# Routing on the normalised rows ahead of gain and bias, and a head whose first two weight units run in pairs

## The reference, cut to what matters

```
x  = layer_norm(x, emb_ln_g, emb_ln_b)
m  = token_mixer(x)        # z = x @ w_in + b_in: attention, spatial gating, convolution; gates; w_o
x1 = layer_norm(ALPHA * x + m, ln1_g, ln1_b)
s  = sigmoid(x1 @ w_router)                    # 16 experts
sb = (s + b_router) in 4 groups of 4
group = argmax(sum of the best 2 of sb)        # one group per token
idx   = best 2 experts of that group
w     = s[idx] / sum(s[idx])
y  = sum over the 2 experts of w * ((silu(x1 @ w_e1) * (x1 @ w_e3)) @ w_e2)
out = layer_norm(ALPHA * x1 + y, ln2_g, ln2_b)
```

## Time and profile before

| | |
|---|---|
| median of 3 runs | 828.07 us (827.59 to 828.2) |
| the profiled execution | 827.32 us, span 825.5 us |
| TensorE matmul busy | 750.6 us, 91% of the span |
| VectorE, ScalarE, GpSimd busy | 628.9, 426.8, 94.6 us |
| mean granted TensorE clock | 0.959 of full |

### The profile page before, as it was taken

How to read it: one execution, slowest core, us unless ns; L and a number is a source line. 1 busy time by engine, 2 the same in 40 slices (tenths; PEclk the granted TensorE clock), 3 DMA queues, 4 the chain that set the end, 5 groups by cost and what they waited for, 6 DMA issues and landing times.

```text
span 825.5 us, 10954 instructions
## 1 busy us (share of the span) xinstructions
PE 750.6 (91%) x3544; PEld 617.0 (75%) x3544; DVE 628.9 (76%) x902; ACT 426.8 (52%) x569; POOL 94.6 (11%) x91
## 2 busy tenths in 40 slices
PE   3899999999999999999999649999999999999930
PEld 3688877888888888888888438888888888888720
DVE  4589986666588658434578658999999999999948
ACT  4622134547322246232321508888888888888711
POOL 3100000000000000000113310111111111112606
PEclk9899999999999999999999859999999999999965
DMA  8833657221323332333596627999999999996252
GB/s 256 241 93 93 193 146 197 70 60 53 95 83 102 102 98 81 104 96 97 191 371 234 250 97 244 362 349 367 368 379 365 388 376 372 370 370 230 82 202 104
DMA packets 129103, 171.95 MB, mean 208 GB/s; under 512 B 15338, under 2 KB 67270, under 8 KB 129046
## 3 DMA queue, kind: packets, MB, share of 16 engines
q1 hardware_dynamic: 121440, 154.95, 55.5%
q0 software_dynamic: 6688, 15.79, 5.5%
q10 hardware_dynamic: 934, 0.69, 0.3%
HBM read 164.05 MB, written 15.97 MB: 218 GB/s over the span
## 4 chain that ended last, share of the span: by engine, by line
PE 78%; DVE 11%; DMA 4%; ACT 3%; issue 2%; SPq 2%; ACTq 0%; POOL 0%; DVEq 0%; POOLq 0%
PE bank L1642 23%; PE bank L1643 23%; PE bank L1644 23%; PE bank L1855 2%; DMA raw<-in_w_in_dram 2%; DVE w_lo L940 2%; SPq L561 1%; DVE conv L1004 1%; PE bank L1818 1%; DVE conv_odd L1004 1%; PE bank L1680 1%; PE bank L1870 1%; DMA w_s_in<-in_w_s_dram 1%; PE bank L1690 1%; PE bank L1637 1%
## 5 line engine op out<-in xcount | busy, mean ns | idle before, releaser
L940 DVE TENSOR_TENSOR w_lo<-raw,w_hi 128x1024 fp32r<-128x1024 f32 x104 | 126.3, 1220 | 81.2 <-ACT w_hi L670 80.7
L670 ACT CAST w_hi<-raw 128x1024 fp32r<-128x1024 f32 x104 | 108.2, 1049 | 105.6 <-PE bank L1644 92.6
L1642 PE MATMUL bank<-xT_hi,w_hi 128*128 128x512 f32 x352 | 138.6, 394 | 1.1 <-DVE vs L1093 1.0
L1643 PE MATMUL bank<-xT_lo,w_hi 128*128 128x512 f32 x352 | 137.5, 391 | 0.0
L1644 PE MATMUL bank<-xT_hi,w_lo 128*128 128x512 f32 x352 | 137.3, 390 | 0.0
L1642 PE MATMUL bank<-w_hi,xgT_hi 128*128 128x512 f32 x192 | 79.1, 412 | 1.6 <-DVE xgT_lo L1392 1.6
L1642 PEld LDWEIGHTS bank<-xT_hi,w_hi 128*128 128x128 f32 x352 | 66.4, 189 | 15.7 <-issue 2.1
L1644 PEld LDWEIGHTS bank<-xT_hi,w_lo 128*128 128x128 f32 x352 | 66.4, 188 | 14.0
L1644 PE MATMUL bank<-w_hi,xgT_lo 128*128 128x512 f32 x192 | 76.7, 400 | 0.0
L1643 PE MATMUL bank<-w_lo,xgT_hi 128*128 128x512 f32 x192 | 76.4, 398 | 0.0
L1643 PEld LDWEIGHTS bank<-xT_lo,w_hi 128*128 128x128 f32 x352 | 66.4, 189 | 13.4
(11 more groups left out here) (251 smaller groups left out, 1582.5 us busy)
## 6 DMA issues: line engine op xcount, KB each, us to landing
raw_more<-in_w_e_dram SPq DMA_DIRECT2D x48, 512.0 KB, 6.7
raw<-in_w_e_dram SPq DMA_DIRECT2D x48, 512.0 KB, 7.0
raw_late<-in_w_e_dram SPq DMA_DIRECT2D x48, 512.0 KB, 6.4
raw_rows<-in_w_e_dram SPq DMA_DIRECT2D x48, 512.0 KB, 7.2
raw<-in_w_in_dram SPq DMA_DIRECT2D x28, 512.0 KB, 5.6
raw<-in_w_gate_dram SPq DMA_DIRECT2D x24, 512.0 KB, 3.7
raw<-in_w_o_dram SPq DMA_DIRECT2D x8, 512.0 KB, 3.8
x_scratch<-x_in SPq DMA_DIRECT2D x4, 512.0 KB, 6.7
```

The lines of the kernel that those rows point to most:

```text
L670: act.copy(hi_slot(j), raw_slot(j)).then_inc(hi_cast, 1)
L940: dve.tensor_tensor(lo_slot(j), raw_slot(j), hi_slot(j).bitcast(F32), ALU.subtract).then_inc(lo_cast, 1)
L1642: pe.matmul(out, hi_l, hi_r, start=start, stop=False)
L1643: pe.matmul(out, hi_l, lo_r, start=False, stop=False)
```

## The change

*Head.* The six weight units are issued without a wait for the rows. `ln1_g` and `ln1_b` are loaded as rows too, on GpSimd's queue, and `w_s` has a semaphore of its own. TensorE turns chunks 0 to 6 of the first two tiles before it waits for the rows. VectorE makes both parts of unit 0; the high parts of x's odd chunks are made by VectorE, those of even chunks by ScalarE. The first two outputs use banks 0 and 1, and their units are run chunk by chunk in turns; `w_s` is turned behind them. SyncE no longer waits for the stored x and `w_s` before the bias loads.

*Routing.* ScalarE writes the normalised rows to a new tile `x1n`; the transposes and the router read that, with `w_router` multiplied by `ln1_g` and a row `ln1_b @ w_router` added. The transposes of the first tiles stand between the `w_o` products of the later ones. The scores come out with tokens on partitions: the turned rows are the stationary operand, 16 columns move. All of `ln1_g` and `ln1_b` is applied by VectorE beside that. `router_bias` is eight matmuls of 16 columns, `route` one and eight. Ranks come from tables of pairwise comparisons that don't wait for each other, summed by one reduction. Between the two casts ahead of the routing stand six small VectorE operations (clearings, constants, `info[..., 0]`). The position counts are float32r. Two of the four expert casts are moved behind the routing. GpSimd's passes (`ln1_b`, ALPHA) are gone; ALPHA is taken in VectorE's first of the two last adds (L1482).

```
-        sp.wait_ge(rows_loaded, 16 * 9)
-                sp.wait_ge(x0_stored, 16 * TT)
-                sp.wait_ge(*drained("w_s"))
...
-        cast_hi(0)
         act.wait_ge(*drained("vectors"))
...
-            if c:
+            if c % 2:
                 act.wait_ge(x0T_full, c)
-                act.copy(xT_hi[:, c - 1, :], conv[:, (c - 1) % WC, :]).then_inc(x0T_hi_done, 1)
+                act.copy(xT_hi[:, c - 1, :], conv[:, (c - 1) % WC, :]).then_inc(x0T_hi_act, 1)
+            if c == 1:
+                cast_hi(1)
...
+        dve.tensor_copy(hi_slot(0), raw_slot(0)).then_inc(first_hi, 1)
+            if c % 2:
+                dve.wait_ge(x0T_full, c + 1)
+                dve.tensor_copy(xT_hi[:, c, :], conv[:, c % WC, :]).then_inc(x0T_hi_dve, 1)
...
+        first_units(0, (0, 1))
+        first_units(1, (0, 1))
+        for c in range(2, DC):
+            for u in range(2):
+                first_units(u, (c,))
+        pe.wait_ge(w_s_loaded, 16)
         turn("w_s", lambda k: w_s[:, k, :])
...
+        normalise(0)
+        normalise(1)
+        copy_x1T(0)
+        normalise(2)
+        copy_x1T(1)
+        normalise(3)
+        cast_hi(U_MOE)
+        copy_x1T(2)
+        cast_hi(U_MOE + 1)
+        copy_x1T(3)
         act.wait_ge(*filled("router"))
+        act.activation(r_s[:].rearrange("p t g e -> p (t g e)"), bank("router")[:, 0:TT * EXPERTS],
+                       ACT.Sigmoid).then_inc(frees("router"), 1)
+        cast_hi(U_MOE + 2)
+        cast_hi(U_MOE + 3)
...
         def scale_x1(t):
-            if t % 2:
+            dve.wait_ge(normalised, 2 * t + 2)
+            dve.tensor_tensor(x1[:, t, :], x1n[:, t % 2, :], ln1_g[:], ALU.mult).then_inc(scaled, 1)
+            dve.tensor_tensor(x1[:, t, :], x1[:, t, :], ln1_b[:], ALU.add).then_inc(x1_ready[t], 1)
...
         def ranks(rank, beats, value):
             for d in range(1, 4):
                 k = 4 - d
+                over = 5 * (k - 1) + 1
+                dve.tensor_tensor(beats[:, :, 4 * d:4 * d + over:5], value[:, :, 0:k], value[:, :, d:4], ALU.is_ge)
+                dve.tensor_tensor(beats[:, :, d:d + over:5], value[:, :, d:4], value[:, :, 0:k], ALU.is_gt)
+            dve.wait_ge(dve_step, step(6))
+            dve.tensor_reduce(rank, beats.rearrange("p m (i j) -> p m i j", j=4), AX.X, ALU.add)
...
+        cast_lo(U_MOE)
...
+        cast_lo(U_MOE + 1)
...
         make_onehot(0, 0)
         make_onehot(1, 1)
         slot_tokens(0, 0, None, keep=False)
         slot_tokens(1, 1, None, keep=False)
+        cast_lo(U_MOE + 2)
+        cast_lo(U_MOE + 3)
...
+        mix_out(0)
+        mix_out(1)
+        router_bias()
+        mix_out(2)
+        turn_x1(0)
+        mix_out(3)
+        turn_x1(1)
+        route(0)
+        turn_x1(2)
+        route(1)
+        turn_x1(3)
+        route(2)
+        route(3)
...
-        pe.matmul(bank("position")[:, 0:80], before, sel, start=True, stop=False)
+        pe.matmul(bank("position")[:, 0:80], before_r[:], sel, start=True, stop=False)
...
+        pool.wait_ge(x1_stored, 16 * TT)
         pool.memset(xg[:], 0.0).then_inc(pool_step, 1)
-        pool.wait_ge(x1_stored, 16 * TT)
...
-        for t in range(TT):
-            pool.tensor_scalar(x1[:, t, :], x1[:, t, :], ALPHA, None, ALU.mult).then_inc(x1_scaled, 1)
```

More of the change, by code:

```diff
@@ new lines, in _ @@
+        dve.tensor_scalar(token_one[:], token, 1.0, None, ALU.add).then_inc(dve_step, 1)
+        dve.tensor_copy(info[..., 0], tokens).then_inc(dve_step, 1)
+        cast_lo(U_MOE + 1)
+        dve.wait_ge(dve_step, step(6))
+        dve.wait_ge(*drained("router"))
+        dve.tensor_tensor(r_sb[:], r_s[:], per_tile(b_router[:]), ALU.add).then_inc(dve_step, 1)
+        dve.wait_ge(dve_step, step())
+        ranks(r_rank[:].rearrange("p t g e -> p (t g) e"), r_beats[:], r_sb[:].rearrange("p t g e -> p (t g) e"))
@@ L1328, in _ @@
[L1328 removed]
+        dve.tensor_tensor(r_kth[..., 3:4], r_kth[..., 2:3], sel[..., 2:3], ALU.add).then_inc(dve_step, 1)
+        dve.wait_ge(dve_step, step(2))
         dve.tensor_tensor(gates[:], r_tmp[:].rearrange("p t g e -> p t (g e)"),
                           w_inv[:].unsqueeze(2).to_broadcast([P] + by_expert), ALU.mult).then_inc(dve_step, 1)
[L1331 removed]
@@ L1332, in _ @@
-        dve.wait_ge(dve_step, step(3))
+        dve.scalar_tensor_tensor(out=info[..., 1], in0=r_kth[:].rearrange("p t g e -> p t (g e)"), scalar=float(T),
+                                 in1=token_one[:].unsqueeze(2).to_broadcast([P] + by_expert), op0=ALU.mult,
+                                 op1=ALU.add).then_inc(dve_step, 1)
+        dve.wait_ge(dve_step, step(2))
         dve.tensor_copy(info[..., 2], gates[:]).then_inc(dve_step, 1)
-        tt(info[..., 1], position[:], tokens, ALU.add)
+        dve.wait_ge(*filled("position"))
@@ L1346, in _ @@
-        dve.tensor_scalar(position[:], position[:], -1.0, None, ALU.add).then_inc(routed, 1)
+        dve.tensor_tensor(info[..., 3], gates[:], info[..., 2].bitcast(F32), ALU.subtract).then_inc(dve_step, 1)
         dve.wait_ge(routed, 1)
@@ new lines, in turn_x1, with route @@
+        def turn_x1(t):
+            for half in range(2):
+                pe.wait_ge(normalised, 2 * t + half + 1)
+                turn(("x1T", t, half), lambda k: x1n[:, t % 2, (4 * half + k) * P:(4 * half + k + 1) * P])
+        def route(t):
+            if t == 0:
+                open_bank("router")
+                pe.wait_ge(router_scaled, 4)
+                pe.wait_ge(*drained("router_bias"))
+            scores = bank("router")[:, t * EXPERTS:(t + 1) * EXPERTS]
+            pe.matmul(scores, ones[0:1, :], router_row[0:1, :], start=True, stop=False)
+            for half in range(2):
+                pe.wait_ge(*drained(("x1T", t, half)))
+                for c in range(4 * half, 4 * half + 4):
+                    o = pe.matmul(scores, x1T[:, c, tokens_of(t)], w_routed[:, c, :], start=False, stop=c == DC - 1)
+            if t == TT - 1:
+                o.then_inc(fills("router"), 1)
```

277 lines of the change are left out of this document (147 added, 130 removed).

## The result

The changed kernel takes 815.8 us (median of 4 runs, 814.27 to 817.13) against 827.83 beside it: a ratio of 0.9851, 95% interval 0.9838 to 0.9863. That is 12.0 us faster, inside the range of 807 to 817, 4.3 us above the forecast of 811.5, and outside the band of 808 to 814.5 that had the largest chance: it lies where the first rival had put it. The gain that the steps had summed to was 16.6. The profiled execution took 817.13 us, its span 815.3.

What follows compares the result with a forecast made beforehand. TensorE was taken as busy nearly throughout, leaving head, routing and end to give time: 827.3 - 6.0 (head) - 10.6 (routing) - 0 (end) = 810.7 us, as a median 811.5; 8-in-10 range 807 to 817.

Steps and rivals of the forecast that it cites:

- the first rival: Routing gives less: gather at loaded price (+3.4), comparisons 0.2 apart (+1.3) or router products at lower clock; 813 to 816, chance 0.13.
- Head: Ahead of unit 2: first matmul at 18.6 instead of 25.21 us, unit 2 at 31.2 instead of 37.5; -6.0 us.
- So the gain is carried along: Up to 437 us: TensorE had under 3 us of idle, so the head's 6.0 us would persist.
- The path to `r_sb`: Routing, last tile's variance to `r_sb`: ScalarE's casts and copies set the pace; start 466.1 instead of 473.34 us, -7.2.
- so I leave it at 0.23: Routing: each new router product takes 0.23 us, as the old ones did; 0.9 us for the last four.
- The root: Routing, after tile 3's variance: the root takes 1.0 us, from an undisturbed 0.55 rather than the 1.46 seen.
- Ranks and choice: Routing: `r_sb` to choice takes 3.0 us instead of 5.3 (-2.3); choice to one-hot 1.7 instead of 3.3 (-1.5).
- The gather: Routing, after one-hot: it took 3.4 us with quiet DMA and now meets the end of weight traffic; +0.4 us.
- (2): Head gives only 2 to 3 us: rows or x late behind weight units, or long low clock; 814.5 to 820, chance 0.12.
- (3): Head gives more: earlier bias loads remove part of 3 us idle, low clock costs nothing; 805 to 809, chance 0.10.
- (4): Experts are bound by DMA, not TensorE, so only the head's gain stays; 821, chance 0.04.
- (5): Slower: TensorE's clock stays low into the units, 0.2 us more per matmul; 831 if five units, chance 0.04.

Runs made afterwards that it cites:

- head only: Kernel before with only the change's edits ahead of unit 2, first layer norm and routing as before: 823.14 us, ratio 0.9943.
- copies first: Changed kernel with ScalarE copying tile 2's turned rows before normalising tile 3, and two expert casts moved later: 815.54 us, ratio 0.9850.
- fillers: Changed kernel with eight idle wide products added behind route(1), tile 3's turns and route(2): 817.49 us, ratio 0.9866.

## Why the forecast was right, and where it was off

Second profiles of both kernels, stage by stage, in us; the forecast's figures are those of its own steps:

| stage | forecast | measured |
|---|---|---|
| to unit 2 | -6.0 | -5.61 (36.91 to 31.30) |
| units 2 to 68 | 0 | +1.26 |
| unit 68 to tile 3's variance | +1.6 | +1.29 |
| variance to `r_sb` | -8.8 (16.95 to 8.1) | -2.88 (16.81 to 13.93) |
| `r_sb` to one-hot | -3.8 | -3.54 (8.61 to 5.07) |
| one-hot to first expert product | +0.4 | -0.16 |
| first 24 expert products | 0 | +0.84 |
| the other experts' products | 0 | -2.24 and -0.13 |
| sum | -16.6 | -11.17 |

- **Head.** The mechanism was right; the size came out by two errors that cancel. Without the half clock it is more: in *head only* and in four later kernels, with the same head and a granted clock of 1.00 from 17 to 26 us, unit 2 starts at 29.8 to 30.1 instead of 31.3 and 31.5. The forecast had allowed 0.3 us for it, and the changed kernel's two profiles pay about 1.4, a little over the 1.2 that it gave as the full price (two later kernels with such a stretch start unit 2 at 30.7 and 31.0). The better start (17.87, forecast 18.6) pays for that. "So the gain is carried along" failed: 1.3 us of it went by unit 68, and the 64-byte tile alone loses 1.2 there.
- **The path to `r_sb`** is the step that failed: "so I leave it at 0.23" for the router's products and, with it, "From here ScalarE sets the pace". At full clock the new products are as forecast (1.96 us for a tile's 16 records, so 0.98 for its last four products against 0.9). But the first rival's condition, products at the lower clock, came true for all of `route(2)` and `route(3)` and for the turns of tile 3, not just for the last four. From 456.87 on TensorE was the bound: turns 1.97, then twice a bias row and a route, 4.1 each, nothing idle between. By ScalarE's last copy, done at 461.34, and the forecast's 1.5 us behind it `r_sb` would have started at 462.8; it started at 467.33. That is 4.5 us. The clock accounts for them: this stretch of TensorE took 10.1 us, and at full clock its pieces take 1.07 for the turns and 2.28 for a bias row and a route (*copies first*, 449.52 to 451.80), 5.6 in all. It is an upper bound, since at full clock TensorE would wait for some of ScalarE's copies; my expectation for *fillers* counted 3.6.
- **The root.** ScalarE's last copy itself came 1.4 us later than forecast (461.34 - 453.39 = 7.95 behind the variance instead of 6.6), from the root: the forecast had "1.0 us, from the undisturbed one", and it took 2.6 from the variance to ScalarE's start, 1.51 and 0.89 of them on GpSimd. I had taken the undisturbed 0.55 because GpSimd's own passes over x1 were to go. They went, and it stayed slow. In the changed kernel it overlaps VectorE's multiply and add over 1,024 values; in the head, with VectorE on statistics, it still takes 0.55 and 0.27. The traces say more than this pair. In all 14 profiles the 128x1 root took 0.55 to 0.57 us wherever VectorE ran nothing beside it, or statistics, or the add with one operand in PSUM (446.33 is such a one), and 1.42 to 1.54 us wherever an operation of VectorE with two tensors in SBUF overlapped it for 0.99 us or more (those that met one for under 0.1 us took 0.55). The Trainium skill has in Advanced Engine Details and Errata, section GPSIMD Details, that GpSimd shares a read and a write interface with VectorE and conflicts with its operations that have two SBUF inputs; the rows agree with it. No run took the overlap away from this root. At half clock the late root costs little: TensorE was done with `route(1)` at 456.63 and idle for only 0.24 us before the turns, and behind them it never waited, so an earlier root could have gained no more than that.
- **Ranks and choice.** `r_sb` to the end of the choice 3.16 in the first profile (467.33 to 470.49) against 3.0; choice to one-hot 1.92 against 1.7. The comparisons start 0.13 to 0.10 apart at 48 to 16 values, each 0.18 to 0.25 long. So the rule that I had cited from the Trainium skill, VectorE: DVE Perf Modes, section The DRAIN you can't avoid, by which they would have cost 0.2 each, did not bind: leaving out the semaphores did gain. The same section says that a next operation that is not held starts earlier, which I had passed over, and that is what these rows show. (Twelve comparisons at 0.2 are 2.4 us, 1.1 more than the 1.3 counted, not 1.3 more.)
- **The gather** took 3.36 us, against 3.40, with the DMA share at 0.08 beside it (0.14 before); the 0.4 for traffic was not needed.
- **Experts.** The forecast counted nothing there. Places of tiles gave 2.1, the half clock took 0.8.
- **The rivals.** (1), with its products at the low clock and its 813 to 816, is what happened. Its other two conditions did not. (2) did not: the rows cost no wait (TensorE turned them at 12.62), and the clock was at half for 3.4 us, not for two units. (3) did not either: the idle time between units 2 and 68 shrank from 3.1 to 1.7 us, but it does so in the kernel before with the 64-byte tile too. (4) is excluded: the experts' stage moved with the operands' places, and the routing's gain stayed. (5) did not occur: the clock was back at 22.8. Its figure was wrong besides: five units are 120 matmuls, at 0.2 us each 24 us beyond the forecast, 835.5 and not 831.
- **The signs.** From tile 3's variance to the first expert product it took 29.1 us (453.39 to 482.48), where about 24 was to show that the working is right.

The one step on the path to `r_sb` is 5.9 us short, more than the whole miss between the two profiles (16.6 - 11.2 = 5.4). The rest nearly cancels: what was lost by the places up to unit 68 (1.3) and at half clock in the first expert products (0.8) came back in the experts (2.1 by the places). None of these three was in the forecast, so that they cancel is luck. Between the medians the miss is 4.3.

## What to carry to other kernels

Before judging an edit by a per cent, look at what it does to the addresses: here one unused tile of 64 bytes was worth 2.8 us, and moving the large matmul operands to multiples of 512 bytes 7 us, over half of what the whole change gave. Compare the distance from start to start of the same products in the same stage; if that moved, the places moved. And a stretch of narrow products and turns must be priced at both clock levels, since here TensorE being busy throughout did not keep it at the full one; idle wide products gained 2.5 us where TensorE waited; where it was the bound, ten of them gained nothing and twenty cost some 3 us.

## What the runs showed of the hardware

- The distance between float32r matmuls of 128x512 at full clock goes with the operands' offset in the partition: 0.2266 to 0.2281 us with both at a multiple of 128 bytes (but for 120 to 200 us, where it reaches 0.229), 0.2287 to 0.233 with one at 64, up to 0.2332 at 32. In the second executions of both kernels each stage's mean came again within 0.0003 us.
- In the changed kernels TensorE's clock fell from 1.00 to 0.50 4.5 to 6.3 us after the last w_o product, with narrow products and turns and next to no idle time between, and 13 us after it with twenty idle wide products among them.
- A GpSimd operation on one value per partition took 0.55 to 0.57 us by itself, beside VectorE's statistics or beside its add from PSUM, and 1.42 to 1.54 beside VectorE's operations on two tensors in SBUF, in all 14 profiles; the one that follows it took 0.27 alone and 0.89 in the changed kernel's routing.
- Independent VectorE comparisons of 16 to 48 values start 0.10 to 0.13 us apart, of 4 to 12 values 0.07 to 0.09.
